# Scaled one-hot rows for four tokens in one comparison and one product

## The reference, cut to what matters

```
eidx = jnp.take_along_axis(cidx, pos, axis=-1)          # first index * 128 + second index
gate = jax.nn.softmax(top, axis=-1)
act  = jax.nn.gelu(jnp.einsum('td,thkd->thk', xb, expert_u[eidx]))
out  = jnp.einsum('thk,thkd->td', gate * act, expert_v[eidx])
```

## Time and profile before

| what | value |
|---|---|
| time, median of 3 runs | 2932.06 us (2929.46 to 2933.86) |
| span of the profiled execution | 2925.2 us |
| PE busy | 2751.4 us, 94% |
| PEld busy | 2471.9 us, 85% |
| DVE busy | 1666.4 us, 57% |
| ACT busy | 1290.2 us, 44% |
| POOL busy | 1183.3 us, 40% |

### The profile page before, as it was taken

The page is one execution under the profiler, slowest core; times in us unless marked ns, Lnnn a source line. Parts: engine busy times, 40 slices in busy tenths (PEclk is TensorE's granted clock), DMA queues, the critical chain, the costliest instruction groups (busy, mean ns, idle before and its releaser), DMA issues.

```text
span 2925.2 us, 52632 instructions
## 1 busy us (share of the span) xinstructions
PE 2751.4 (94%) x16304; PEld 2471.9 (85%) x16304; DVE 1666.4 (57%) x4177; ACT 1290.2 (44%) x2533; POOL 1183.3 (40%) x1524
## 2 busy tenths in 40 slices
PE   7979989979989999999998999997989999999997
PEld 7868879968889999998886888986879999999886
DVE  2253447999943333334666546999963333333665
ACT  4344534656644444443222534665654444443222
POOL 6513336874444444442000145793444444443000
PEclk9989999989999999999999999998999999999999
DMA  5214422324464544454655422343464445444562
GB/s 196 91 65 173 172 86 85 134 99 174 187 221 162 176 165 161 161 183 143 197 179 189 153 101 94 115 135 138 172 227 171 168 167 183 161 161 151 179 197 104
DMA packets 138432, 451.92 MB, mean 154 GB/s; under 512 B 6561, under 2 KB 90529, under 8 KB 95598
## 3 DMA queue, kind: packets, MB, share of 16 engines
q1 hardware_dynamic: 128046, 391.59, 39.3%
q0 software_dynamic: 10304, 59.26, 5.1%
HBM read 401.15 MB, written 49.68 MB: 154 GB/s over the span
## 4 chain that ended last, share of the span: by engine, by line
PE 67%; DVE 22%; issue 6%; DVEq 2%; ACT 2%; POOL 1%; DMA 1%; POOLq 0%; ACTq 0%
PE psum L893 24%; PE psum L715 8%; PE psum L898 8%; PE psum L685 8%; PE psum L686 8%; PE psum L687 8%; DVE shared L1627 5%; DVE arena L1527 1%; DVE arena L1525 1%; DVE arena L1530 1%; DVE arena L1582 1%; DVE arena L1623 1%; DVE arena L1524 1%; DVEq L1627 1%; DVE arena L1529 1%
## 5 line engine op out<-in xcount | busy, mean ns | idle before, releaser
L599 POOL TENSOR_TENSOR w_split<-w_ring,w_split 128x256 fp32r<-128x256 f32 x1152 | 920.0, 806 | 835.4 <-ACT w_split L1160 769.5
L685 PE MATMUL psum<-uT_split,w_split 128*128 128x320 f32 x2560 | 819.8, 320 | 28.4 <-POOL w_split L599 17.2
L1160 ACT ACTIVATE w_split<-w_ring 128x256 fp32r<-128x256 f32 x1152 | 476.4, 418 | 821.8 <-PE psum L687 802.8
L687 PE MATMUL psum<-uT_split,w_split 128*128 128x320 f32 x2560 | 797.2, 311 | 0.0
L686 PE MATMUL psum<-uT_split,w_split 128*128 128x320 f32 x2560 | 797.2, 311 | 0.0
L893 PE MATMUL psum<-v_hl,p_hl 128*128 128x512 f32 x3072 | 741.5, 390 | 0.0
L893 PEld LDWEIGHTS psum<-v_hl,p_hl 128*128 128x128 f32 x3072 | 570.9, 188 | 111.9
L1648 DVE TENSOR_TENSOR v_hl<-w_ring,v_hl 128x1024 fp32r<-128x1024 f32 x256 | 314.2, 1227 | 530.3 <-ACT v_hl L1230 530.3
L685 PEld LDWEIGHTS psum<-uT_split,w_split 128*128 128x128 f32 x2560 | 487.4, 190 | 52.1 <-POOL w_split L599 29.2
L686 PEld LDWEIGHTS psum<-uT_split,w_split 128*128 128x128 f32 x2560 | 487.7, 191 | 5.5
L687 PEld LDWEIGHTS psum<-uT_split,w_split 128*128 128x128 f32 x2560 | 486.6, 190 | 0.0
(11 more groups left out here) (233 smaller groups left out, 1948.8 us busy)
## 6 DMA issues: line engine op xcount, KB each, us to landing
w_ring<-peer_u SPq DMA_DIRECT2D x128, 1024.0 KB, 4.9
w_ring<-peer_v SPq DMA_DIRECT2D x128, 1024.0 KB, 6.3
gates<-w_ring POOLq DMA_DIRECT2D x40, 1024.0 KB, 5.8
arena<-gates SPq DMA_DIRECT2D x32, 1280.0 KB, 9.9
w_ring<-w_pq SPq DMA_DIRECT2D x8, 2048.0 KB, 7.6
w_ring<-w_qk SPq DMA_DIRECT2D x4, 2048.0 KB, 9.7
w_ring<-w_vo SPq DMA_DIRECT2D x4, 2048.0 KB, 7.7
w_ring<-w_xk SPq DMA_DIRECT2D x4, 2048.0 KB, 11.2
```

Of the source, the lines that this page charges most:

```text
L599: pool.tensor_tensor(wq[:, q, 1], quarter(raw, m, q), wq[:, q, 0].bitcast(F32), ALU.subtract).then_inc(w_lo_ready, 1)
L685: pe.matmul(bank[:, 0:TOK], hi, uT_hi[:, k, :], start=k == 0, stop=False)
L687: last = pe.matmul(bank[:, 0:TOK], lo, uT_hi[:, k, :], start=False, stop=k == KD - 1)
L1160: act.activation(wq[:, q, 0], quarter(raw, m, q), ACT.Copy).then_inc(w_hi_ready, 1)
```

## The change

Per group of four tokens DVE now issues three tensor_tensor instructions of 128x512: the comparison of `iota` with the first index into `oh`, the comparison with the second index into `ohJ` (as before, now second), and the product of `oh` with the gate, in place. The four tensor_scalar instructions go. The first comparison raises a new semaphore, `lanes_ready`, for which the product waits on the same engine, with the comparison into `ohJ` between them. `oh_ready` is raised once a group instead of four times, and PE's wait counts accordingly.

```
-                            pe.wait_ge(oh_ready, i * 64 + (TOK * l + 16 * r + 4 * g + 4))
+                            pe.wait_ge(oh_ready, i * 16 + (80 * l + 4 * r + g + 1))
...
-                            dve.tensor_tensor(ohJ[:, 4 * (g % 2):4 * (g % 2) + 4, :], iota.unsqueeze(1).to_broadcast([P, 4, P]),
-                                              slots[:, 1, bass.ds(i * 64 + c, 4)].unsqueeze(2).to_broadcast([P, 4, P]),
+                            half, tok = slice(4 * (g % 2), 4 * (g % 2) + 4), bass.ds(i * 64 + c, 4)
+                            lanes = iota.unsqueeze(1).to_broadcast([P, 4, P])
+                            dve.tensor_tensor(oh[:, half, :], lanes, slots[:, 0, tok].unsqueeze(2).to_broadcast([P, 4, P]),
+                                              ALU.is_equal).then_inc(lanes_ready, 1)
+                            dve.tensor_tensor(ohJ[:, half, :], lanes, slots[:, 1, tok].unsqueeze(2).to_broadcast([P, 4, P]),
                                               ALU.is_equal)
-                        ti, tg = slots[:, 0, bass.ds(i * 64 + c, 1)], slots[:, 2, bass.ds(i * 64 + c, 1)]
-                        dve.tensor_scalar(oh[:, c % 8, :], iota, ti, tg, ALU.is_equal, ALU.mult).then_inc(oh_ready, 1)
+                            dve.wait_ge(lanes_ready, i * 16 + (80 * l + c // 4 + 1))
+                            dve.tensor_tensor(oh[:, half, :], oh[:, half, :], slots[:, 2, tok].unsqueeze(2).to_broadcast([P, 4, P]),
+                                              ALU.mult).then_inc(oh_ready, 1)
```

More of the change, by code:

```diff
@@ L359, in build @@
         mx_ready, p_ready, pooled = (sem(n) for n in ("mx_ready", "p_ready", "pooled"))
-        top_ready, exp_ready, picked_ready, oh_ready = (
-            sem(n) for n in ("top_ready", "exp_ready", "picked_ready", "oh_ready"))
+        top_ready, exp_ready, picked_ready, oh_ready, lanes_ready = (
+            sem(n) for n in ("top_ready", "exp_ready", "picked_ready", "oh_ready", "lanes_ready"))
         w_hi_ready, w_lo_ready, quarter_used = (sem(n) for n in ("w_hi_ready", "w_lo_ready", "quarter_used"))
```

## The result

| | us |
|---|---|
| before, median (beside the changed kernel) | 2932.4 |
| changed, median | 2958.8 (2956.8 to 2964.7) |
| ratio | 1.0099, 95% interval 1.0084 to 1.0114 |
| predicted | 2965, range 2942 to 2986 |

The change makes the kernel slower by 26 us by the medians, 29 by the ratio (25 to 33 by its interval). In each of the four runs of the changed kernel the time is 1.7 us above the span of its own core. In the forecast it stands on both sides and drops out.

A forecast was written before the change was run, and what follows sets the result against it. DVE, busy 40.00 us of 40 in stage gb, was taken as the bound. Terms of 14.4 + 8.4 - 6.5 = +16.3 us a layer, +33 for two, took the time from 2932.1 to 2965 us, range 2942 to 2986.

The forecast's parts named there:

- DVE's own time: DVE in gb: a group goes from 1.62 to 1.80 us, +14.4 us a layer.
- POOL's 76 meetings: POOL's 76 instructions a layer in gb each cost DVE 0.53 us instead of 0.42, +8.4 us a layer.
- The group with the store: Groups in gb with POOL's gate store: 0.18 us extra instead of 0.54, 18 times, -6.5 us a layer.
- The wait at nothing: The product's wait for lanes_ready on DVE is hidden by the second comparison and costs nothing.
- the price without cover: If the second comparison failed to hide the product's wait on DVE: 0.12 us a group, 9.6 us a layer.
- The sum: Stage gb: 14.4 + 8.4 - 6.5 = +16.3 us a layer, +33 us for two, time 2965 us.
- a change of the stage's length goes straight into the span: What follows gb waits for DVE and the stored gates, so the stage's change passes straight into the span.
- (1): POOL no longer gets in between DVE's long instructions in gb: -28 us a layer, 2877 us; chance 0.06.
- (2): DVE's instructions run end to start, own time +0: +1.9 us a layer, 2936 us; chance 0.05.
- (3): POOL's instruction behind the DMA gets SBUF early, 0.65 us extra: 8.5 us a layer more, 2982 us; chance 0.09.
- (4): The product's wait for lanes_ready on DVE shows: +9.6 us a layer, 2984 us; chance 0.09.
- (5): TensorE's clock falls to 1.2 GHz as PE's share drops to 76%: +113 us a layer, 3158 us; chance 0.02.

The follow-up runs named there:

- e1: Changed kernel with POOL's lower parts of the weights in gb cut to 4 columns of 256 in 19 of 20 blocks a layer: 2875.5 us.
- e6: Kernel before, with the lower parts of the weights in gb made by DVE ahead of each group instead of by POOL: 2895.1 us.
- e7: Changed kernel, with the lower parts of the weights in gb made by DVE ahead of each group instead of by POOL: 2922.9 us.
- e2: Kernel before with POOL's lower parts of the weights in gb cut to 4 columns of 256 in 19 of 20 blocks a layer: 2871.7 us.
- e4: Changed kernel with the 40 stores of the gates issued by ACT instead of POOL: 2948.5 us, ratio to before 1.0069.
- e3: Changed kernel with the comparison into ohJ moved in front, so the product comes right behind the comparison it waits for: 2981.5 us.

## Why the prediction was right

*DVE's own time, +0.18 us a group:* quiet groups take 1.81 against 1.62; e1 shows the 1.81 alone, and the pair e6 and e7 the difference, 2.14 against 1.96. Measured 14.5 us a layer (80 x 0.18), predicted 14.4.

*POOL's 76 meetings at 0.53 instead of 0.42:* a met group is 2.34, 0.53 over the quiet 1.81, as predicted. e1 and e2 show that POOL's work, and nothing else, makes the two kernels slower than 1.8 us a group. The Trainium skill, "SBUF — State Buffer", section "SBUF: two separate sides", has a rule for it: one pair of ports is shared by DVE and GpSimd, and whoever comes first owns it for a whole instruction; a DVE instruction with two inputs in SBUF counts, but only against a GpSimd one that reads SBUF. The trace agrees for the long instructions: 1.21 us for a comparison that meets L578, 0.68 for one beside a DMA alone. For the 128x4 instructions of e1 it shows no wait of DVE, though they read SBUF too. That the ports are what the two engines share is the skill's account; the runs show the exclusion and its price.

*The group with the store:* 2.56 against the predicted 2.52, 0.22 over a usual one instead of 0.54 before. In e4 the stores by ACT take it away: behind the first two blocks every group takes 2.34. The reason that I gave, that the L599 behind the DMA owns the way to SBUF from about the DMA's start, is not shown: in e1 the instruction behind the DMA lets the comparison at 703.61 pass and ends 0.05 us after it. In the changed kernel the product that starts at 728.62 has to wait, though L578 starts only at 728.73; how the order of the two is decided stays open.

*The wait at nothing:* right. A quiet group takes three times 0.60 us, which leaves no room for a wait, and e3 shows the wait by taking the cover away. Only the price without cover was too low.

*The sum:* the stage grows by 17.6 us in layer 0 and 18.2 in layer 1, for the predicted 16.3. The store's 0.22 in place of 0.18 makes 0.7 us of the difference, and the groups of 2.79 to 2.90 in the first blocks most of the rest. The time grows by 26 (29 by the ratio), for 33. One step of the prediction was wrong, that a change of the stage's length goes straight into the span: what comes behind the stage does not simply shift with DVE's end. SP's issues there, before and then after:

```profile
824.98 0.34 SPq L501 DMA_DIRECT2D w_ring<-peer_v  x1
833.91 0.41 SPq L503 DMA_DIRECT2D arena<-gates  x1
```
```profile
848.93 0.34 SPq L480 DMA_DIRECT2D w_ring<-peer_v  x1
856.32 0.41 SPq L482 DMA_DIRECT2D arena<-gates  x1
```

The load of the first gates goes out 11.0 us after DVE's last memset started before (822.90), 8.2 after it now (848.13). The last store is issued 0.60 us behind the load of `peer_v` before and 1.45 us now, and the load of the gates follows the store by 8.3 and 5.9 us. That the longer lead over the store makes it land sooner fits these rows, but no run shows it. Counted from the last product of PE, the first `uv` product comes 2.5 us earlier in layer 0 and 1.3 in layer 1, and that last product itself trails DVE by 0.4 us less: some 4.6 us given back, 31 us left of 35.8, inside the interval of 25 to 33. The two errors, 3.2 us too little for the stages and 4.6 too much behind them, have opposite signs: that the total came so near is in part luck. The spans of the two profiles differ by 37.8 us instead; 7.6 us of that is there when `gb` of layer 0 starts, at 650.8 before and 658.4 after (650.7 in e3, 652.4 in e4, 655.7 in e1, all with the same instructions up to there): that part is not the change's.

*The rivals:* POOL gets in every time (1), the starts overlap (2), the instruction behind the DMA does not get SBUF early (3), the wait does not show (4), and the clock stays at 1.00 (5). PE's busy share is 33.71 of 40, 84%; my 76% set 1.78 us against 2.34, where the 94% before stands for 1.93 us of 2.05. The range of the forecast itself was added up wrongly: 2965 - 17 - 5 is 2943 and not 2945, and no term gives its upper end, 2972. The stated range, 2942 to 2986, holds both.

## What to carry to other kernels

Count an engine's cost from start to start in a quiet stretch and in a crowded one, and not by its mean duration: here the mean of 462 ns was 0.26 us from start to start, 0.08 that lie under the next instruction, and the rest POOL. Before long instructions replace short ones, price the streams (128 columns with both operations in 0.26 us against 512 with one in 0.60) and what every meeting with the other engine will cost at the new length. Work that GpSimd did beside a full VectorE was not free here: 128x256 cost 0.42 to 0.53 us a time, 128x4 nothing that the rows show. If VectorE can do such work in less than a meeting costs (0.33 us here), try it there, and try the stores on a queue that nothing of GpSimd waits behind.

## What was not expected of the hardware

Of a wait for the instruction right in front, beside an address out of a register, e3 shows 0.15 us from that instruction's end to the start, where one without such an address had 0.04. The two differ in the instruction as well, so that the address is the cause is not shown.
